# Even tokens first in the dilated attention branch, with its two wide dilations as two diagonal blocks per head

## The reference

```python
h = _layer_norm(x) * (1.0 + sc1) + sh1
proj = h @ w_in                        # qa, ka, va, qd, kd, vd, gates
out_a = _global_gqa(qa, ka, va)        # 8 heads, 2 of keys and values, head width 64
for g, (window, dilation) in enumerate(((128, 1), (512, 4), (2048, 16))):
    # 4 heads each: query t sees keys t + dilation * (-reach .. reach), reach = window / (2 * dilation)
    sc = q.k * scale - slope * abs(offset)
    o[g], lse[g] = softmax(sc) @ v, logsumexp(sc)
out_b = sum(softmax(lse over g)[g] * o[g])
mix = (sigmoid(gate_a) * (out_a @ w_branch_a) + sigmoid(gate_b) * (out_b @ w_branch_b)) @ w_out
```

## Time and profile before

| what | value |
|---|---|
| median of three runs | 1681.82 us (1681.4 to 1682.25) |
| the profiled execution's own time | 1681.89 us |
| its span | 1680.0 us |
| PE busy | 1546.3 us, 92% |
| DVE, ACT busy | 543.4 us, 350.6 us |
| mean granted TensorE clock | 0.961 |
| moved by DMA | 463.30 MB, 276 GB/s |

### The profile page before, as it was taken

One profiled execution on the slowest core, in us unless ns is written; L12 is line 12 of the kernel. 1 busy time (PEld: TensorE's weight loads), 2 busy tenths in 40 slices (PEclk: granted clock), 3 DMA queues, 4 the chain that ended last, 5 costly groups with the idle time before them and its releaser, 6 DMA issues.

```text
span 1680.0 us, 17060 instructions
## 1 busy us (share of the span) xinstructions
PE 1546.3 (92%) x7298; PEld 867.4 (52%) x7298; DVE 543.4 (32%) x950; ACT 350.6 (21%) x775; POOL 16.2 (1%) x34
## 2 busy tenths in 40 slices
PE   5999998799979999979999998999988999899895
PEld 2777676454357677645435444443424775444332
DVE  1542333622266134362224034221103363412113
ACT  3113240311121223031113122110102243201011
POOL 0000000000000000000000000000001000000000
PEclk8999999799989999979998998999998999899998
DMA  9775344589837542458983624799999422799995
GB/s 383 283 287 213 151 170 181 225 337 410 354 119 275 191 191 71 180 225 342 411 349 131 216 96 183 327 426 428 428 428 398 169 100 106 306 428 426 428 428 231
DMA packets 34697, 463.30 MB, mean 276 GB/s; under 512 B 4432, under 2 KB 4560, under 8 KB 6288
## 3 DMA queue, kind: packets, MB, share of 16 engines
q1 hardware_dynamic: 31376, 447.32, 65.1%
q0 software_dynamic: 3232, 14.71, 2.7%
HBM read 458.87 MB, written 3.15 MB: 275 GB/s over the span
## 4 chain that ended last, share of the span: by engine, by line
PE 76%; DMA 16%; DVE 5%; ACT 2%; issue 1%; SPq 0%; DVEq 0%; ACTq 0%
PE work L669 15%; PE work L501 12%; DMA ring<-in_stream 10%; PE work L492 9%; PE work L722 7%; PE acc L501 6%; DMA area<-in_stream 6%; PE acc L492 5%; PE work L626 4%; PE acc L704 2%; PE work L1139 2%; PE acc L1285 2%; PE acc L826 1%; PE work L938 1%; PE work L687 1%
## 5 line engine op out<-in xcount | busy, mean ns | idle before, releaser
L669 PE MATMUL work<-ring,area 128*64 128x512 f32 x832 | 186.2, 594 | 12.1 <-DMA ring<-in_stream 12.0
L501 PE MATMUL work<-ht_sb,ring 128*128 128x256 f32 x640 | 143.4, 384 | 1.1 <-DMA ring<-in_stream 1.1
L501 PEld LDWEIGHTS work<-ht_sb,ring 128*128 128x128 f32 x640 | 121.7, 192 | 22.6 <-issue 4.4
L669 PEld LDWEIGHTS work<-ring,area 128*64 128x64 f32 x832 | 58.3, 137 | 131.5 <-issue 108.4
L492 PE MATMUL work<-ring,ht_sb 128*128 128x512 f32 (+1 forms) x320 | 118.8, 530 | 5.1 <-ACT ht_sb L1405 2.6
L2153 DVE SCALAR_TENSOR_TENSOR area<-area,comb_slot,work 128x256 f32<-128x256 f32 (+1 forms) x32 | 19.6, 614 | 301.0 <-ACT area L1468 301.0
L501 PE MATMUL acc<-ht_sb,ring 128*128 128x256 f32 x512 | 114.0, 381 | 0.2 <-DMA ring<-in_stream 0.2
L669 PE MATMUL work<-area 128*64 128x512 f32 x448 | 100.9, 594 | 7.2 <-DMA area<-in_stream 7.2
L501 PEld LDWEIGHTS acc<-ht_sb,ring 128*128 128x128 f32 x512 | 96.1, 190 | 17.2 <-issue 4.0
L2165 DVE TENSOR_TENSOR area_r<-work,area_r 128x512 fp32r<-128x512 f32 x64 | 44.2, 691 | 170.2 <-ACT area_r L1476 137.7
L492 PEld LDWEIGHTS work<-ring,ht_sb 128*128 128x128 f32 x320 | 62.2, 197 | 56.1 <-issue 47.8
(11 more groups left out here) (278 smaller groups left out, 1796.4 us busy)
## 6 DMA issues: line engine op xcount, KB each, us to landing
ring<-in_stream SPq DMA_DIRECT2D x138, 2048.0 KB, 12.0
area<-in_stream SPq DMA_DIRECT2D x55, 2048.0 KB, 12.8
cst<-in_stream SPq DMA_DIRECT2D x19, 2048.0 KB, 16.6
ln_sb<-in_ln_vecs POOLq DMA_DIRECT2D x8, 1024.0 KB, 11.5
rel_rows<-mt_sb POOLq DMA_DIRECT2D x1, 2048.0 KB, 49.7
area<-rel_rows POOLq DMA_DIRECT2D x16, 128.0 KB, 4.2
cst<-in_consts POOLq DMA_DIRECT2D x1, 1529.5 KB, 9.5
x_sb<-in_x SPq DMA_DIRECT2D x1, 1024.0 KB, 16.3
```

Of the source, the lines that this page charges most:

```text
L501: ins = pe.matmul(dst, w[:, k, c0:c0 + n], src[:, k0 + k, :], start=k == 0, stop=k == ks - 1)
L669: ins = pe.matmul(banks[half][e * CAP:(e + 1) * CAP, :], tokens[:, k, at:at + CAP], w[:, kk, e, half * W:(half + 1) * W], start=k == 0, st ...
```

## The change

Inside the dilated branch, queries, keys and values stand in the order of even tokens, then odd tokens.

- Queries and keys (`QD`, `KDT`) are put in that order by ACT's copies out of PSUM: 6 copies per layer read every second float (`by_parity` in place of `pairs`), and write contiguously.
- Values: the products of b = 5 and of the second half of b = 4 take every second token of `HT` as stationary operand (`natural_by_parity`); 128 columns as before, now 8 bytes apart.
- Groups g = 1 and 2 compute only the two blocks of 128 queries by 128 keys of one parity each: scores move 128 keys in place of 256, 4 transposes in place of 8, values move 128 columns in place of 256. The table of distances has 512, 256 and 256 columns for the three groups in place of 3 x 512 (with 512 spare, so that nothing behind it moves). DVE's addition and the copies of flipped probabilities are 256 wide in place of 512, maximum and exponential cover 512 keys in place of 768. Group 0 keeps its full size.
- `take_values(4)` and `(5)` write the result back in the tokens' order (every second float of `OUTT`).

The global branch, the order on every engine, the waits and the stream of slots stay as they are.

```diff
+            def natural_by_parity(dst, w, c0, n, r, last=None):
+
+                tokens = HT.rearrange("p k (i r) -> p k r i", r=2)
+                for k in range(KD):
+                    ins = pe.matmul(dst, tokens[:, k, r, :], w[:, k, c0:c0 + n], start=k == 0, stop=k == KD - 1)
                 if last is not None:
                     ins.then_inc(last, 1)
...
-                    elif b in (0, 5):
+                    elif b == 0:
                         for t in range(TT):
                             one_natural(s, 0, W, t, last_use=t == 1)
+                    elif b == 5:
+                        for r in range(2):
+                            j, bank, filled = begin()
+                            natural_by_parity(bank[:, :], w, 0, W, r, filled)
+                        release(s)
...
-                            natural(bank[:, t * T:(t + 1) * T], HT, w, 0 if b == 1 else T, T, t, filled if t else None)
+                            if b == 1:
+                                natural(bank[:, t * T:(t + 1) * T], HT, w, 0, T, t, filled if t else None)
+                            else:
+                                natural_by_parity(bank[:, t * T:(t + 1) * T], w, T, T, t, filled if t else None)
...
-                def scores(q, k):
+                def scores(q, k, diagonal=False):
 
                     for qt in range(TT):
+                        n = P if diagonal else T
+                        keys = slice(qt * P, (qt + 1) * P) if diagonal else slice(0, T)
                         for e in range(2):
                             a = HD * e
-                            ins = pe.matmul(work[e][:, qt * T:(qt + 1) * T], q[a:a + HD, qt * P:(qt + 1) * P], k[a:a + HD, :],
+                            ins = pe.matmul(work[e][:, qt * n:(qt + 1) * n], q[a:a + HD, qt * P:(qt + 1) * P], k[a:a + HD, keys],
                                             start=True, stop=True)
...
+                            if diagonal:
+                                ins = pe.transpose(banks[e][:, kt * P:(kt + 1) * P], two[e][:, kt, :], ident)
+                            else:
+                                for qt in range(TT):
+                                    ins = pe.transpose(banks[e][:, kt * T + qt * P:kt * T + (qt + 1) * P],
+                                                       two[e][:, qt, kt * P:(kt + 1) * P], ident)
...
+                        at, n = (kt * P, P) if diagonal else (0, T)
                         for e in range(2):
-                            pe.matmul(bank[HD * e:HD * (e + 1), 0:T], v[e][:, kt, :], p[e][:, kt, :],
+                            pe.matmul(bank[HD * e:HD * (e + 1), at:at + n], v[e][:, kt, :], p[e][:, kt, :],
                                       start=first and kt == 0, stop=False)
                         for e in range(2):
-                            ins = pe.matmul(bank[HD * e:HD * (e + 1), T:2 * T], ones[:, 0:HD], p[e][:, kt, :],
+                            ins = pe.matmul(bank[HD * e:HD * (e + 1), T + at:T + at + n], ones[:, 0:HD], p[e][:, kt, :],
                                             start=False, stop=last and kt == TT - 1)
...
+            def by_parity(dst):
+
+                return dict(dst=dst.rearrange("p a (r i) -> p a r i", r=2),
+                            src=lambda b: b[:, :].rearrange("p (a i r) -> p a r i", a=2, r=2))
...
-                copy_out(**pairs(QD[:, 0:2, :]), scale=SCALE)
+                copy_out(**by_parity(QD[:, 0:2, :]), scale=SCALE)
...
+                    if at < 4:
+                        dve.tensor_tensor(OUTT[:, at, :], acc[3][:, 0:T], INV, ALU.mult).then_inc(values_taken, 1)
+                    else:
+                        by_token = OUTT[:, at, :].rearrange("p (i r) -> p r i", r=2)
+                        dve.tensor_tensor(by_token, acc[3][:, 0:T].rearrange("p (r i) -> p r i", r=2),
+                                          INV.rearrange("p (r i) -> p r i", r=2), ALU.mult).then_inc(values_taken, 1)
...
-                    dist = const("dist").rearrange("p (g q k) -> p g q k", g=NG, q=TT)[:, g]
+                    dist = const(f"dist{g}").rearrange("p (q k) -> p q k", q=TT)
                     for e in range(2):
-                        ins = dve.scalar_tensor_tensor(PB_B[p][e][:, :, g, :], dist, -alibi_slope(4 * g + 2 * p + e),
-                                                       work[e][:, :].rearrange("p (q k) -> p q k", q=TT), ALU.mult, ALU.add)
+                        ins = dve.scalar_tensor_tensor(PB_B[p][e][:, :, KEYS_B[g]], dist, -alibi_slope(4 * g + 2 * p + e),
+                                                       work[e][:, 0:CONST[f"dist{g}"][1]].rearrange("p (q k) -> p q k", q=TT),
+                                                       ALU.mult, ALU.add)
```

More of the change, by code:

```diff
@@ L493, in natural @@
                                     start=k == 0, stop=k == KD - 1)
+                if last is not None:
+                    ins.then_inc(last, 1)
+            def natural_by_parity(dst, w, c0, n, r, last=None):
+                tokens = HT.rearrange("p k (i r) -> p k r i", r=2)
+                for k in range(KD):
+                    ins = pe.matmul(dst, tokens[:, k, r, :], w[:, k, c0:c0 + n], start=k == 0, stop=k == KD - 1)
                 if last is not None:
@@ L939, in scores, with flip_probs @@
                                             start=True, stop=True)
                     ins.then_inc(scores_ready, 1)
-                def flip_probs(two, banks):
+                def flip_probs(two, banks, diagonal=False):
                     for e in range(2):
                         for kt in range(TT):
-                            for qt in range(TT):
-                                ins = pe.transpose(banks[e][:, kt * T + qt * P:kt * T + (qt + 1) * P],
-                                                   two[e][:, qt, kt * P:(kt + 1) * P], ident)
+                            if diagonal:
[4 more added lines that the diff above has]
+                                                       two[e][:, qt, kt * P:(kt + 1) * P], ident)
@@ L949, in flip_probs, with values @@
                     ins.then_inc(flip_ready, 1)
-                def values(v, p, first, last):
+                def values(v, p, first, last, diagonal=False):
                     bank = acc[3]
                     for kt in range(TT):
+                        at, n = (kt * P, P) if diagonal else (0, T)
                         for e in range(2):
-                            pe.matmul(bank[HD * e:HD * (e + 1), 0:T], v[e][:, kt, :], p[e][:, kt, :],
+                            pe.matmul(bank[HD * e:HD * (e + 1), at:at + n], v[e][:, kt, :], p[e][:, kt, :],
@@ L981, in scores_b @@
                         pe.wait_ge(scores_taken, C.seen(scores_taken))
-                    scores(QD[:, 2 * g + p, :], KDT[:, 2 * g + p, :])
+                    scores(QD[:, 2 * g + p, :], KDT[:, 2 * g + p, :], g > 0)
                 def flip_b(p, g):
                     banks = [work[0], work[1]] if (p, g) == (1, 1) else [work[2], work[3]]
-                    flip_probs([PB_B[p][e][:, :, g, :] for e in range(2)], banks)
+                    flip_probs([PB_B[p][e][:, :, KEYS_B[g]] for e in range(2)], banks, g > 0)
                 def values_b(p, g):
@@ L994, in values_b @@
                     c = 128 + (4 * g + 2 * p) * HD
-                    values([VN[:, :, c:c + HD], VN[:, :, c + HD:c + 2 * HD]], [PT_B[e][:, g] for e in range(2)],
-                           g == 0, g == NG - 1)
+                    values([VN[:, :, c:c + HD], VN[:, :, c + HD:c + 2 * HD]], [PT_B[e][g] for e in range(2)],
+                           g == 0, g == NG - 1, g > 0)
                 pe.wait_ge(qk_ready, C.seen(qk_ready))
@@ L1666, in take_flipped @@
                     act.wait_ge(flip_ready, C.seen(flip_ready))
-                    act.activation(dst.rearrange("p k q -> p (k q)"), work[3][:, :], ACT.Copy).then_inc(pt_by_act, 1)
+                    n = TT * dst.shape[2]
+                    act.activation(dst.rearrange("p k q -> p (k q)"), work[3][:, 0:n], ACT.Copy).then_inc(pt_by_act, 1)
                 gate(0)
@@ L2321, in _ @@
                     dve.wait_ge(flip_ready, C.seen(flip_ready))
-                    take_flipped(PT_B[0][:, g], work[2]).then_inc(pt_by_dve, 1)
+                    take_flipped(PT_B[0][g], work[2]).then_inc(pt_by_dve, 1)
                     scores_b(1, g)
@@ L2589, in constants @@
     far = [np.where((dist % d == 0) & (dist <= w // (2 * d) * d), dist, FAR) for w, d in B_GROUPS]
-    put("dist", np.stack([by_tile(m) for m in far], 1))
+    by_parity = np.concatenate([t[0::2], t[1::2]])
+    far = [m[by_parity][:, by_parity] for m in far]
+    put("dist0", by_tile(far[0]))
+    for g in (1, 2):
+        put(f"dist{g}", np.stack([far[g][r * P:(r + 1) * P, r * P:(r + 1) * P] for r in range(2)], 1))
     put("later", (i[:, None] > i[None, :]) & (i[:, None] // CHUNK == i[None, :] // CHUNK))
```

37 lines of the change are left out of this document (19 added, 18 removed).

## The result

The changed kernel takes 1671.18 us, the median of six runs (1669.37 to 1675.82), against 1681.89 us of the kernel before in the same rounds (1679.73 to 1682.69): the ratio is 0.994, interval 0.9926 to 0.9955. The profiled execution took 1672.25 us, with a span of 1670.5.

A forecast was written before the change was run, and what follows sets the result against it. PE was taken as the bound up to gate(7), whose release lets pa's and pb's transfers be requested. Savings of 4.30 + 4.66 - 1.7 = 7.3 us from 1681.9 gave 1674.6 us, range 1671.5 to 1679.5.

The forecast's parts named there:

- What counts and what doesn't: Dilated attention: PE savings before gate(7) count fully, 4.30 us per layer; 2.15 after it count only through layer 1's division.
- Unit prices: PE savings per unit of groups 1 and 2: scores 0.43 us, transposes 0.43, values 0.86.
- Transposes and values: Per unit, 4 fewer transposes save 0.43 us; values moving 128 columns save 0.86 us.
- Scores: Per unit, moving 128 keys saves 0.43 us, bounds 0 and 0.43; the rival of no saving had chance 0.15.
- Projection and copies: Values' projection with loads 8 bytes apart and ACT's strided PSUM copies cost 0; rival of slow loads, 1688.7 us, chance 0.07.
- Layer 1's end: In layer 1, pa's products no longer wait 0.36 us for DVE's division, so that layer gives 4.66 us.
- The clock: Idle PE ahead of pa: a new clock fall in layer 1 costs 1.7 us, bounds none and 1.7; layer 0 unchanged.

The follow-up runs named there:

- after_again: The changed kernel run once more without any edit: 1672.37 us, ratio 0.994 to the kernel before.
- wide_p0: Changed kernel with values' products of (0,1) and (0,2), ahead of gate(7), moving 256 columns, same instruction count: 1676.38 us, ratio 0.9957 to the kernel before.
- wide_p1: Changed kernel with values' products of (1,1) and (1,2), behind gate(7), moving 256 columns, same instruction count: 1670.99 us, ratio 0.9925 to the kernel before.
- scores_full: Changed kernel with scores of the wide dilations moving all 256 keys, same instructions: 1672.2 us, ratio 0.9932 to the kernel before.
- pad: Changed kernel with 32 unread 1x1 products on PE in layer 0's idle stretch ahead of pa: 1671.02 us, ratio 0.9935 to the kernel before.
- early_0: Changed kernel with gate(7) earlier in PE's order, ahead of the transposes of (0,2), in layer 0 alone: 1667.5 us, ratio 0.9905 to the kernel before.
- twice_p0: Changed kernel with values' products of (0,1) and (0,2), ahead of gate(7), issued twice: 1678.02 us, ratio 0.9969 to the kernel before.
- filler: Changed kernel with unread 128x128 by 256 products ahead of PE's wait for pa and pb, 14 in layer 0, 4 in layer 1: 1677.01 us, ratio 0.9969.
- twice_p1: Changed kernel with values' products of (1,1) and (1,2), behind gate(7), issued twice: 1677.75 us, ratio 0.998 to the kernel before.

## Why the prediction held, and where it was off

*What counts and what doesn't.* Right. Work ahead of gate(7) counts in full; work behind it counts not at all in layer 0 and in layer 1 only as far as the division holds pb's products back, shown by the two runs at full width. The forecast gave 4.30 us to each layer up to there; the unit prices gave 4.18, the stretches 3.8 and 4.6. What parts the stretches from the 4.18 lies in transfers. In layer 0 it is the two that took 0.21 us longer each. In layer 1 the time from pb's request to the first load behind it was 8.62 us before and 8.25 after; in the kernel before, one instruction packet lies in that transfer and in the changed one none:

```profile
q8 instruction: 1, 0.02, 0.7%
```

This line is of the DMA queues by kind, 668.4 to 676.7 us of the kernel before.

*Unit prices.* Transposes and values within 0.02 us. Scores were the open one, 0 or 0.43; they gave 0.41, and back to 1.06 us when they moved 256 keys. By the Trainium skill, page "TensorEngine Tiling (Array Packing)", section "Tiling Modes", tiles load and multiply in parallel; the trace agrees, with 0.65 us for four steps of 128 keys, where eight loads one after the other (0.11 us each) would alone take 0.88.

*Projection and copies.* Right at 0. By the Trainium skill, page "Advanced Engine Details and Errata", section "Memory Cachelines", two hits on a line of 16 bytes are enough and one is not; the loads agree: 196 ns at 8 bytes and 319 at 16. Of PSUM, where its lines are of 8 bytes and it warns of any gaps for matmuls, ACT's copies with every second float show no loss (597 ns, as before).

*Layer 1's end.* The waiting for the division went as forecast: from pa's first product to the next stage's transposes it took 727.33 - 667.89 = 59.44 us against 736.74 - 676.97 = 59.77 before, 0.33 for the 0.36.

*The clock.* This is the term that was mis-sized. I charged 1.7 us for a fall in layer 1, reading an idle stretch of 2.33 us in the earlier trace rows as its like; after 1.99 us of idle the clock stood at 1.00, and so it did in the other seven kernels that idle there. In layer 0 I took no change; the fall cost 0.7 us more (61.80 against 61.12). Together that is 1.7 - 0.7 = 1.0 us of the missing 3.4.

*The rest.* In the profiled executions the stage of experts and the projection behind it, from 314.73 to 584.25 against 317.36 to 588.69, were 1.8 us shorter (269.52 us against 271.33), though nothing in them was changed. It isn't one lucky execution of the changed kernel: after_again took 269.70 us there, and the kernels wide_p0, wide_p1, scores_full, pad and early_0 took 269.0 to 270.2. But the kernel before has one trace only, and no experiment took these stages apart: the cause is open.

The 9.5 us between the two spans are made up of 3.8 and 4.6 in the stretches, 0.3 behind pa in layer 1 and these 1.8, less 0.7 for the clock in layer 0 and 0.5 ahead of the first values; 0.1 comes behind. The last 1.2 of the 10.7 lie between this pair of executions and the medians. So the 1.8 us and these 1.2 were not forecast, and that the result came out at the low end of the range and not near its middle is owed to them and to the fall of the clock that didn't come. The range was drawn too high at its low end for the same reason, since a kernel whose own runs scatter over 6 us can't be held to 3 us below the forecast.

## What to carry to other kernels

Follow the chain back through the transfer to the release that lets it be requested. Work ahead of that release counts, work behind it is free until the transfer lands, and the busy share of an engine tells neither. If an engine idles ahead of a transfer, move the release, not the work: moving one gate in one layer gave 4 to 6 us (1667.5 against 1671 to 1672, ratio 0.9905 against 0.994), no less than removing 4 us of products had given in that layer (3.8). And to undo a part for a test, keep the number of instructions; issuing work twice changed more than the work.

## What the runs showed of the hardware

- A stationary operand with its columns 8 bytes apart loads like a contiguous one (196 against 190 ns recorded); 16 bytes apart it takes 319 ns, and 64 bytes no more than that (300).
- One 16 KB packet of instructions (0.02 MB of queue q8) within a saturated transfer that PE waited for went with 1.2 to 1.3 us more: in layer 0, 13.28 to 13.50 us in four kernels with the packet, 12.01 to 12.34 in ten without. In layer 1 it was 9.01 us in place of 8.03 once.
- Adding instructions on PE cost 2 to 5 us more than their work explained in three runs, while 32 tiny ones in the idle stretch cost nothing. In the trace with values issued twice for p = 1, 2.2 us are placed in the two stretches up to pa, where the two transfers are longer, and 2.3 in the stages between; that execution was the fastest of nine and lost only 0.9 us in all against after_again's, so what makes the median 5.4 us longer is open.
- An idle stretch of 0.96 us, which the kernels have at the same place, was followed by a fall of the clock in two executions and not in the others; idle stretches of 1.27 to 2.02 us ahead of pa in layer 1 by none in eight; at a third place, waits of 0.62 and 1.33 us (twice_p0, filler) by a fall and one of 0.55 (twice_p1) by none. Of such short ones nothing can be forecast from one trace.
